# Activation chunks laid 1552 instead of 1536 bytes apart

## The reference

```
h = h + w * gate * f(rmsnorm(h) * (1 + scale) + shift)     # w = 1/2 for an FFN, 1 for the mixer
swiglu(x) = (silu(x @ w_gate) * (x @ w_up)) @ w_down       # hidden width 2816
layer 0 mixer: neighbourhood attention (8 heads) and grouped-query attention (8 / 2 heads), one q/k/v projection
layer 1 mixer: u, v = split(gelu(x @ w_in)); (u * mix_positions(rmsnorm(v))) @ w_out
```

## Time and profile before

| | |
|---|---|
| median of 3 runs | 1677.5 us (1674.35 to 1678.1) |
| the profiled execution's own time | 1673.53 us |
| its span, first to last instruction | 1671.7 us |
| mean granted clock of TensorE | 0.974 of full |
| read from main memory | 258.75 MB, 156 GB/s over the span |

### The profile page before, as it was taken

The page is one execution under the profiler, slowest core; times in us unless marked ns, Lnnn a source line. Parts: engine busy times, 40 slices in busy tenths (PEclk is TensorE's granted clock), DMA queues, the critical chain, the costliest instruction groups (busy, mean ns, idle before and its releaser), DMA issues.

```text
span 1671.7 us, 23837 instructions
## 1 busy us (share of the span) xinstructions
PE 1610.1 (96%) x9487; PEld 1539.8 (92%) x9487; DVE 1037.7 (62%) x1296; ACT 578.4 (35%) x751; POOL 84.2 (5%) x48
## 2 busy tenths in 40 slices
PE   8899999988899899999989999998999998999998
PEld 3899999988756799999989999998999998999998
DVE  3577768858754767767966676796854434434323
ACT  2423332252454342322243333224534334333222
POOL 1200000035000100000010000001000010000000
PEclk9999999989999899999989999998999998999999
DMA  9655557535201435555734555675433332343431
GB/s 319 173 189 170 200 178 255 171 112 189 76 1 38 151 125 196 183 203 202 251 126 143 184 196 181 210 242 176 152 102 126 126 126 80 122 134 118 143 128 67
DMA packets 190291, 261.90 MB, mean 157 GB/s; under 512 B 14518, under 2 KB 142102, under 8 KB 190230
## 3 DMA queue, kind: packets, MB, share of 16 engines
q1 hardware_dynamic: 190230, 261.06, 47.1%
HBM read 258.75 MB, written 2.29 MB: 156 GB/s over the span
## 4 chain that ended last, share of the span: by engine, by line
PE 84%; issue 6%; DVE 4%; SPq 2%; ACT 1%; POOL 1%; DMA 1%; POOLq 0%; ACTq 0%; DVEq 0%
PE ps L1104 16%; PE ps L1107 16%; PE ps L1105 16%; PE ps L1050 9%; PE ps L1052 9%; PE ps L1051 9%; DVE macc L776 2%; PE ps L1291 2%; PE ps L1328 1%; SPq L416 1%; PE ps L1164 1%; DMA raw<-ffn_w_gu 1%; POOL sqsum L512 1%; PE ps L1396 1%; PE ps L1117 1%
## 5 line engine op out<-in xcount | busy, mean ns | idle before, releaser
L738 DVE TENSOR_TENSOR w_lo<-raw,w_hi 128x2048 fp32r<-128x2048 f32 x164 | 378.1, 2306 | 279.8 <-ACT w_hi L536 278.8
L1104 PE MATMUL ps<-x_hi,w_hi 128*128 128x384 f32 x1536 | 521.5, 340 | 13.8 <-ACT x_hi L560 9.9
L1105 PE MATMUL ps<-x_hi,w_lo 128*128 128x384 f32 x1536 | 520.3, 339 | 0.0
L1107 PE MATMUL ps<-x_lo,w_hi 128*128 128x384 f32 x1536 | 517.7, 339 | 0.0
L536 ACT ACTIVATE w_hi<-raw 128x2048 fp32r<-128x2048 f32 x169 | 322.9, 1910 | 325.3 <-PE ps L1052 304.4
L1104 PEld LDWEIGHTS ps<-x_hi,w_hi 128*128 128x128 f32 x1536 | 292.4, 190 | 17.9 <-issue 13.3
L776 DVE SCALAR_TENSOR_TENSOR macc<-mraw,cT,macc 128x512 f32<-128x512 f32 x448 | 302.9, 746 | 0.0
L1105 PEld LDWEIGHTS ps<-x_hi,w_lo 128*128 128x128 f32 x1536 | 292.2, 190 | 0.0
L1107 PEld LDWEIGHTS ps<-x_lo,w_hi 128*128 128x128 f32 x1536 | 291.8, 190 | 0.0
L1050 PE MATMUL ps<-act_hi,w_hi 128*128 (+1 forms) x832 | 280.1, 337 | 0.0
L1051 PE MATMUL ps<-act_lo,w_hi 128*128 (+1 forms) x832 | 279.6, 336 | 0.0
(11 more groups left out here) (157 smaller groups left out, 1230.1 us busy)
## 6 DMA issues: line engine op xcount, KB each, us to landing
raw<-ffn_w_gu SPq DMA_DIRECT2D x88, 1024.0 KB, 5.1
mraw<-mod_w SPq DMA_DIRECT2D x66, 1024.0 KB, 7.2
raw<-ffn_w_down SPq DMA_DIRECT2D x44, 1024.0 KB, 4.9
raw<-sgu_w_in SPq DMA_DIRECT2D x16, 1024.0 KB, 5.5
raw<-attn_w_in SPq DMA_DIRECT2D x9, 1024.0 KB, 5.4
raw<-sgu_w_out SPq DMA_DIRECT2D x8, 1024.0 KB, 4.9
mfirst<-mod_w SPq DMA_DIRECT2D x6, 1024.0 KB, 12.8
raw<-attn_w_out SPq DMA_DIRECT2D x4, 1024.0 KB, 4.9
```

What stands on the lines that cost most here:

```text
L738: nc.vector.tensor_tensor(w_lo[q0 % 2][:, :], raw[q0 % 2][:, :], w_hi[q0 % 2][:, :].bitcast(F32), ALU.subtract).then_inc(lo_done, 1)
L1104: mm(out, hi[:, cols], x_hi[:, k, :], start=(k == 0), stop=False)
L1105: mm(out, lo[:, cols], x_hi[:, k, :], start=False, stop=False)
L1107: last = mm(out, hi[:, cols], x_lo[:, k, :], start=False, stop=(k == KD - 1))
```

## The change

The four activation tiles get rows of 388 instead of 384 columns, of which 384 are used, so that a chunk begins 1552 bytes behind the one before it. Chunk k then begins 16k bytes further on, modulo 128, than chunk 0. As 8 x 1552 = 97 x 128, x_lo still begins 64 bytes past a multiple of 128; act_lo begins 32 bytes past one. `sqsum` is no tile of its own any more but chunk 3 of `tmp`, and the two small areas of head sums in it move to its end. The tiles behind sqsum begin 1536 bytes earlier, and those behind x_lo 1280 bytes earlier, both multiples of 128.

```diff
+TP = T + 4
...
-        sqsum = sb("sqsum", [P, T])
+        sqsum = tmp[:, 3, :]
...
-        hms, hrs = sqsum[:, 0:12], sqsum[:, 16:28]
+        hms, hrs = sqsum[:, T - 32:T - 20], sqsum[:, T - 16:T - 4]
...
-        x_hi = sb("x_hi", [P, KD, T], F32R)
-        x_lo = sb("x_lo", [P, KD, T], F32R)
+        x_hi = sb("x_hi", [P, KD, TP], F32R)[:, :, 0:T]
+        x_lo = sb("x_lo", [P, KD, TP], F32R)[:, :, 0:T]
...
-        act_hi = sb("act_hi", [P, KF, T], F32R)
-        act_lo = sb("act_lo", [P, KF, T], F32R)
+        act_hi = sb("act_hi", [P, KF, TP], F32R)[:, :, 0:T]
+        act_lo = sb("act_lo", [P, KF, TP], F32R)[:, :, 0:T]
```

## The result

The changed kernel takes 1686.1 us (median of 4 runs, 1685.4 to 1688.5) against 1676.8 us for the kernel before, a ratio of 1.006, interval 1.0042 to 1.0077: slower by some 9 us, where no change was forecast. The profiled execution takes 1686.2 us with a span of 1684.4 us, 12.7 us over the span of before; the profiled execution of before was one of its quicker ones.

What follows compares the result with a forecast made beforehand. TensorE, busy 96% of the span, was taken to bound the kernel through its matmul pace. The terms summed as 0 + 0 + 0 + 0 on the 1677.5 us median, giving 1677 us, range 1625 to 1705 (likeliest case 1672 to 1682).

Steps and rivals of the forecast that it cites:

- the first term: 384-column matmuls of the panels and output projection: new chunk starts cost 0, bounded by -97 and +50 us.
- moves where the meetings fall, and not how many there are: Moving and weight reads within one matmul, pattern repeating every 128 bytes: a new start leaves the time unchanged.
- The two comparisons in the earlier trace: Operands at both old kinds of place: mraw against mfirst, 379 ns each; h against x_tok transposes, 273 ns each.
- The bounds and the range: Bounds of the unknown chunk-place cost, -97 and +50 us; whole-kernel range 1625 to 1705 us.
- of act likewise: Chunk starts after the change: act chunk k, like x's, begins at 64 + 16k (mod 128).
- Rival A: 384-column matmuls: the 32 extra cycles are meetings of two reads, most new places avoid them; 1593 to 1653 us; chance 0.32.
- Rival B: 384-column matmuls: a chunk beginning inside a wider fetch needs one more; 12 us (1690) or 36 us (1714); chance 0.21.
- Token-major panels: 17 panels with x chunks as weight load, at 113.3 or 117.8 ns: taken as 0, bounds -5.4 to +5.4 us.
- The writers and sqsum: act_hi copies and act_lo subtractions into wider tiles, and sqsum in chunk 3 of tmp: each taken as 0.

Runs made afterwards that it cites:

- the table: Mean steps by shift: against the kernel before, x and act pairs shifted as a whole, another amount per stage; two kernels, 1682.4 and 1684.5 us (before: 1677.9 us).

## Why the prediction was wrong

**The step that failed** is the first term, "I take 0, by the nearest rows", and the reason under it, that moving the start "moves where the meetings fall, and not how many there are". The term measured +1.4 to 1.9 ns on each 384-column matmul, 10.8 us in the gate/up and down stages. The two comparisons in the earlier trace rows couldn't see it: one streams past two-column weights, the other moves only 128 columns, and both compare durations, which in the changed kernel stayed at 340 ns too. The reason fails in its last step: the cost does depend on where the two streams start, between 0 and 3.3 ns (8 cycles) a matmul in the table, and the pattern repeats after 256 bytes, not 128. The bounds and the range held, but through the share given to the rivals and not through the mechanism forecast. (The places were misread in one more point, which changed no sum: "of act likewise" is true of act_hi, while act_lo begins at 32 + 16k.)

**The size.** Over the twelve shifts of the table with one pace the mean excess is 1.1 ns, and jumping between free places cost 1.1 ns more. The changed kernel pays 1.4 to 1.9 ns, less than the sum; so the two aren't simply added, and its exact size is not derived.

**Rival A** had, as far as the places tell, the right nature, two reads that meet, and the wrong sign: it held the old place for a bad one, whereas it is among the best. Its prize of up to 97 us wasn't there: no place got under 416 cycles on the mean. The 0.170 us steps that spoke for it exist in the changed kernel too, as steps of 169 and 170 ns, and others of 178 to 182 ns more than make up for them.

**Rival B** had the right sign, and its lower price, 12 us, is near the 10.8 us measured; but its reason, the chunk's own place, is wrong: the weights' place alone made 22.6 us, with the activations where they were modulo 256.

**Token-major panels.** The two paces of the earlier trace rows were read rightly, the bounds (-5.4 to +5.4 us) held, and the value 0 didn't: +3.5 us, since no panel keeps 113.3 ns when the stationary chunk lies at varying places: before, 12 of the 17 panels ran at 113.3 to 113.5 ns, after, all 17 at 117.9 to 118.4.

**The writers and sqsum** cost nothing, as forecast: the copy to act_hi took 847 against 846 ns, the subtraction for act_lo 958 ns before (L862) and after (L863), and sqsum alone gave 1677.6 against 1677.5 us.

The Trainium skill (SBUF — State Buffer, section Who interferes with whom) gives TensorE two independent ports for moving operand and weights. If that means that neither read slows the other, the measurement differs and decides: with only the weights moved, the step went from 173.3 to 176.7 ns.

## What to carry to other kernels

When matmuls follow each other without a gap, the pace is in the distance of their starts; busy time and mean duration hide it. A place that runs at one constant step is worth protecting: before padding a tile that such float32r matmuls read, work out the place of each of its chunks against the other operand, here modulo 256 bytes, and shift both or neither. A row that lacks the disputed pairing (here a long moving read beside a full weight load) bounds nothing, however equal its two numbers are.

## What the runs showed of the hardware

- At the full clock the start-to-start time of a float32r matmul depends on the place of the moving operand relative to the stationary one, modulo 256 bytes: 173.3, 174.8, 175.6, about 176 or 176.7 ns for 384 columns; at the half clock it is 320 ns at all places seen. With the weights alone moved it is 176.7 ns even while no other engine works.
- One relation (128) ran at 173.3, 174.7 and 176.7 ns, and changed from 176.7 to 173.3 ns at a pause of TensorE of about 2.6 us. The token-major panels of before likewise change between 113.3 and 117.8 ns at pauses. What picks the pace at a start stays open.
- At full clock a matmul of 320, 384 or 448 columns takes 32 cycles more than its columns (37 at 512), and halving the stationary columns at 384 does not change that.
